# Moving operands read in two halves by turns, 16 columns at a time, with operands moved to whole 64-byte lines

## The reference, cut to what matters

```python
def first_block(...):
    n = _rmsnorm(h, pre_mix_norm[l])
    proj = jnp.einsum('btd,dn->btn', n, w_in[l])
    ...
    merged = (sigmoid(gate_a) * einsum('btv,vd->btd', y_gdn, w_branch_gdn[l])
              + sigmoid(gate_b) * einsum('btv,vd->btd', y_dsa, w_branch_dsa[l]))
    mix = jnp.einsum('btd,de->bte', merged, w_out[l])
    h = h + _rmsnorm(mix, post_mix_norm[l])
    n2 = _rmsnorm(h, pre_mlp_norm[l])
    u = jnp.square(jax.nn.relu(jnp.einsum('btd,df->btf', n2, w_up[l])))
    h = h + _rmsnorm(jnp.einsum('btf,fd->btd', u, w_down[l]), post_mlp_norm[l])

def swiglu(x, w_gu, w_down):
    gu = jnp.einsum('bsd,df->bsf', x, w_gu)
    g, u = gu[..., :D_FF_2], gu[..., D_FF_2:]
    return jnp.einsum('bsf,fd->bsd', jax.nn.silu(g) * u, w_down)

def moe_swiglu(x, w_router, w_gu, w_down):          # N_EXPERTS = 8, TOP_K = 2
    ...
    for e in range(N_EXPERTS):
        out = out + gates[..., e:e + 1] * swiglu(x, w_gu[e], w_down[e])
    return out
```

## Time and profile before

| | before |
|---|---|
| median of the runs | 1777.97 us |
| the profiled execution | 1777.92 us, of which the span is 1776.1 us |
| PE busy | 1754.1 us (99%), 11249 matmuls and as many loads |
| DVE busy | 1363.0 us (77%) |
| ACT busy | 1076.1 us (61%) |
| POOL busy | 158.2 us (9%) |
| DMA | 447.90 MB, 252 GB/s over the span |
| mean granted TensorE clock | 0.996 of 2.4 GHz |

### The profile page before, as it was taken

The page is one execution under the profiler, slowest core; times in us unless marked ns, Lnnn a source line. Parts: engine busy times, 40 slices in busy tenths (PEclk is TensorE's granted clock), DMA queues, the critical chain, the costliest instruction groups (busy, mean ns, idle before and its releaser), DMA issues.

```text
span 1776.1 us, 26513 instructions
## 1 busy us (share of the span) xinstructions
PE 1754.1 (99%) x11249; PEld 1579.0 (89%) x11249; DVE 1363.0 (77%) x1591; ACT 1076.1 (61%) x1200; POOL 158.2 (9%) x165
## 2 busy tenths in 40 slices
PE   9999999999999999999999999999999999999997
PEld 8999999999988999998998888888888888888885
DVE  6895598577664667655687899888889898889897
ACT  7754455455544454444446777777777776767774
POOL 1454270000000100000030100000000000000110
PEclk9999999999999999999999999999999999999999
DMA  9342464656556555575463599999999999999994
GB/s 288 119 116 64 124 184 143 211 180 189 181 188 202 190 164 167 183 235 178 132 201 130 202 380 376 380 336 383 372 381 341 385 370 384 332 381 376 379 390 171
DMA packets 265206, 447.90 MB, mean 252 GB/s; under 512 B 11461, under 2 KB 135848, under 8 KB 264952
## 3 DMA queue, kind: packets, MB, share of 16 engines
q1 hardware_dynamic: 263464, 440.36, 71.1%
q0 software_dynamic: 1616, 5.77, 0.8%
HBM read 438.99 MB, written 4.73 MB: 250 GB/s over the span
## 4 chain that ended last, share of the span: by engine, by line
PE 91%; DVE 5%; ACT 2%; issue 1%; DMA 0%; SPq 0%; DVEq 0%; ACTq 0%
PE bank L428 27%; PE bank L430 27%; PE bank L429 27%; DVE ring_r L418 2%; PE bank L3240 1%; ACT hi_ring L403 1%; PE bank L2522 1%; PE bank L3154 1%; PE bank L1348 1%; PE bank L1340 1%; DVE arena L923 1%; PE bank L1832 1%; PE bank L2503 0%; PE bank L2152 0%; PE bank L1817 0%
## 5 line engine op out<-in xcount | busy, mean ns | idle before, releaser
L418 DVE TENSOR_TENSOR ring_r<-ring,hi_ring 128x2048 fp32r<-128x2048 f32 x401 | 905.4, 2284 | 264.7 <-ACT hi_ring L403 264.2
L403 ACT CAST hi_ring<-ring 128x2048 fp32r<-128x2048 f32 (+1 forms) x404 | 757.2, 1904 | 136.3 <-PE bank L430 129.3
L428 PE MATMUL bank<-hi_ring,arena_r 128*128 128x512 f32 (+1 forms) x1526 | 569.2, 373 | 2.0 <-DVE ring_r L418 2.0
L429 PE MATMUL bank<-ring_r,arena_r 128*128 128x512 f32 (+2 forms) x1534 | 567.5, 370 | 0.0
L430 PE MATMUL bank<-hi_ring,arena_r 128*128 128x512 f32 (+1 forms) x1526 | 566.7, 371 | 0.0
L428 PE MATMUL bank<-ring_r,hi_ring 128*128 128x256 f32 (+1 forms) x1400 | 398.9, 285 | 0.0
L430 PE MATMUL bank<-ring_r 128*128 128x256 f32 (+1 forms) x1400 | 395.2, 282 | 0.0
L429 PE MATMUL bank<-ring_r,hi_ring 128*128 128x256 f32 (+1 forms) x1400 | 395.0, 282 | 0.0
L428 PEld LDWEIGHTS bank<-hi_ring,arena_r 128*128 128x128 f32 x1526 | 286.8, 188 | 54.9 <-DVE ring_r L418 4.8
L429 PEld LDWEIGHTS bank<-ring_r,arena_r 128*128 128x128 f32 (+1 forms) x1534 | 287.9, 188 | 51.0
L430 PEld LDWEIGHTS bank<-hi_ring,arena_r 128*128 128x128 f32 x1526 | 286.9, 188 | 50.2
(11 more groups left out here) (436 smaller groups left out, 1572.7 us busy)
## 6 DMA issues: line engine op xcount, KB each, us to landing
ring<-in_w_gu_moe SPq DMA_DIRECT2D x176, 1024.0 KB, 7.3
ring<-in_w_down_moe SPq DMA_DIRECT2D x88, 1024.0 KB, 6.0
ring<-in_w_in SPq DMA_DIRECT2D x31, 1024.0 KB, 5.5
ring<-in_w_gu_dense SPq DMA_DIRECT2D x22, 1024.0 KB, 5.2
ring<-in_w_up SPq DMA_DIRECT2D x16, 1024.0 KB, 5.5
ring<-in_w_down SPq DMA_DIRECT2D x16, 1024.0 KB, 5.0
ring<-in_w_in_a SPq DMA_DIRECT2D x10, 1024.0 KB, 5.8
ring<-in_w_down_dense SPq DMA_DIRECT2D x10, 1024.0 KB, 5.0
```

The lines of the kernel that those rows point to most:

```text
L403: q.e.copy(hi_ring[:, b:b + m], ring[:, a:a + m]).then_inc(*q.did(("hi", of.tag, i)))
L418: q.e.tensor_tensor(ring_r[:, a:a + m], ring[:, a:a + m], hi_ring[:, b:b + m].bitcast(F32), ALU.subtract).then_inc(*q.did(("lo", of.tag, i)))
L428: q.e.matmul(ps, a[0], b[0], start=first, stop=False)
L429: q.e.matmul(ps, a[0], b[1], start=False, stop=False)
```

## The change

`mm3` gives the moving operand and the PSUM output another order of columns. `paired_lines` cuts the columns into two halves, and takes 16 of the first half, 16 of the second, the next 16 of the first, and so on (where their number is a multiple of 128: the shapes 256 and 512, not 272). Every column still goes to its own place in PSUM. 16 columns are 64 bytes.

The other edits move operands. `ARN` grows by 8 columns, so `ring` and `hi_ring` begin 32 bytes later, at 110144: a whole multiple of 64, and 64 past a multiple of 256, and so do all weight blocks. The operands in `arena` that meet weights now begin 192 bytes past a multiple of 256 (for `yg`: 4224 + 4 x 2128 = 12736 = 49 x 256 + 192), and so does `X`, which becomes two packed arrays of 8 x 256 columns, where it had rows of 272. So the moving and the stationary operand of a matmul lie 128 bytes apart modulo 256. Two kinds are exceptions: `nX` keeps its rows of 272 columns, 1088 bytes, so that its distance to the weights goes through 64, 128, 192 and 0 with k in the 256-column shape; and `memT` against two blocks of stationary weights in `arena`.

```diff
-ARN = 26472
+ARN = 26480
...
-    X = Pair(nX.hi[:, :, 0:SEQ], nX.lo[:, :, 0:SEQ])
+    X = Pair(*[shaped(ring_r[:, o:o + 8 * SEQ], (8, SEQ)) for o in (NRAW * BLK + 32, NRAW * BLK + 32 + 8 * SEQ)])
...
+    def paired_lines(a):
+        return a.rearrange("p (h j e) -> p j h e", h=2, e=16) if a.shape[1] % P == 0 else a
+
     def mm3(q, ps, a, b, first, last):
-        q.e.matmul(ps, a[0], b[0], start=first, stop=False)
-        q.e.matmul(ps, a[0], b[1], start=False, stop=False)
-        return q.e.matmul(ps, a[1], b[0], start=False, stop=last)
+        ps, high, low = [paired_lines(v) for v in (ps, b[0], b[1])]
+        q.e.matmul(ps, a[0], high, start=first, stop=False)
+        q.e.matmul(ps, a[0], low, start=False, stop=False)
+        return q.e.matmul(ps, a[1], high, start=False, stop=last)
...
-    yg = pair_at(2176, 8, SEQ)
+    yg = pair_at(2128, 8, SEQ)
...
-    yd = pair_at(8576, 8, SEQ)
+    yd = pair_at(8528, 8, SEQ)
...
-    mg, xin2 = pair_at(13056, 8, SEQ), at(17152, 2, 1024)
+    mg, xin2 = pair_at(13008, 8, SEQ), at(17152, 2, 1024)
...
-    u_, dn = pair_at(2048, 32, SEQ), at(18432, 2, 1024)
+    u_, dn = pair_at(2064, 32, SEQ), at(18456, 2, 1024)
...
-    mix2 = pair_at(6656, 8, SEQ)
+    mix2 = pair_at(6608, 8, SEQ)
...
-    gg = pair_at(6656, 22, SEQ)
+    gg = pair_at(6608, 22, SEQ)
...
-    xs2 = pair_at(10648, 8, 2 * P)
-    hh, hp = at(14744, 2816), pair_at(17560, 22, P)
+    xs2 = pair_at(10640, 8, 2 * P)
+    hh, hp = at(14736, 2816), pair_at(17552, 22, P)
```

More of the change, by code:

```diff
@@ L532, in emit @@
     wT, vn, ktm = AT, D, AT[:, 0:8, :]
-    yg = pair_at(2176, 8, SEQ)
+    yg = pair_at(2128, 8, SEQ)
     rhT, hn = at(6272, P)[0:16, :], [at(o, 512) for o in (13056, 13568, 14080, 16768)]
     sq2 = [flat(AT[:, 2 * j:2 * j + 2, :]) for j in range(8)]
-    aq = at(6528, 8, SEQ)
-    yd = pair_at(8576, 8, SEQ)
+    aq = at(6480, 8, SEQ)
+    yd = pair_at(8528, 8, SEQ)
     iq, ik, ak, av = at(19456, 4, SEQ), at(22528, T), at(22800, 2, T), at(14896, 3, 256)
@@ L551, in emit @@
     mix_sq, x2_sq, r_mix, r_x2 = at(12672, 2, 4), at(12680, 2, 2), at(12684, 2), at(12686, 2)
-    u_, dn = pair_at(2048, 32, SEQ), at(18432, 2, 1024)
-    ut = [at(18432 + SEQ * j, SEQ) for j in range(4)]
-    dn_gain, dn_junk, dn_sq, r_dn = at(21248, 1024), at(20992, 256), at(22272, 2, 4), at(22280, 2)
+    u_, dn = pair_at(2064, 32, SEQ), at(18456, 2, 1024)
+    ut = [at(18456 + SEQ * j, SEQ) for j in range(4)]
+    dn_gain, dn_junk, dn_sq, r_dn = at(21272, 1024), at(21016, 256), at(22296, 2, 4), at(22304, 2)
     xr, xv = at(0, 2, 1024), at(2048, 2, 1024)
@@ L565, in emit @@
     cos2, sin2 = C[:, later + 520:later + 776], C[:, later + 776:later + 1032]
-    mix2 = pair_at(6656, 8, SEQ)
+    mix2 = pair_at(6608, 8, SEQ)
     kx, vx = at(10752, 6, SEQ), at(12288, 2, 12 * 65)
-    memT, memin = pair_at(22376, 8, SEQ), at(2176, 2, 1024)
+    memT, memin = pair_at(22352, 8, SEQ), at(2176, 2, 1024)
     mk_raw = [at(2048, 8, P), at(14368, 8, P)]
@@ L571, in emit @@
     mv_raw = [at(18944, 4, SEQ), at(21304, 4, SEQ)]
-    mv_later = [Pair(at(6656 + 1024 * h, 4, SEQ, of=arena_r), at(o, 4, SEQ, of=arena_r)) for h, o in ((0, 18944), (1, 21304))]
-    ang, kf = at(20480, SEQ), at(20736, SEQ)
+    mv_later = [Pair(at(6608 + 1024 * h, 4, SEQ, of=arena_r), at(o, 4, SEQ, of=arena_r)) for h, o in ((0, 18944), (1, 21304))]
+    ang, kf = at(20504, SEQ), at(20760, SEQ)
     qm = at(13856, 2, SEQ)
@@ L583, in emit @@
     lg, m8b, gt2, oh = at(8192, 2, 8), at(8208, 2, 8), at(8224, 2, 8), at(8240, 2, 2, 8)
-    ixf, sel, ge, posm, cnt = at(8272, 2, 8), at(8288, 2, 8), at(8304, 2, 8), at(8320, 2, 8), at(8336, 8)
+    ixf, sel, ge, posm, cnt = at(9232, 2, 8), at(9176, 2, 8), at(9192, 2, 8), at(9208, 2, 8), at(9224, 8)
     lgT = at(8344, SEQ)
@@ L587, in emit @@
     gs = at(9112, 8)
-    ST = [at(9624 + 256 * j, SEQ, of=arena_r) for j in range(4)]
-    xs2 = pair_at(10648, 8, 2 * P)
-    hh, hp = at(14744, 2816), pair_at(17560, 22, P)
+    ST = [at(9616 + 256 * j, SEQ, of=arena_r) for j in range(4)]
+    xs2 = pair_at(10640, 8, 2 * P)
+    hh, hp = at(14736, 2816), pair_at(17552, 22, P)
     acc, moe_gains = at(2048, 2, 1024), at(0, 2, 1024)
```

## The result

| | before | changed |
|---|---|---|
| median | 1779.08 us (4 runs beside it) | 1822.7 us (4 runs, 1820.7 to 1823.8) |
| ratio | | 1.0243, 95% interval 1.023 to 1.0256 |
| span of the profiled execution | 1776.1 us | 1820.7 us |

The account below looks back on a forecast made before the run. PE's start-to-start matmul distance was taken as the bound; gains of 14.9 (experts), 7.2 (other row products) and 21.1 us (256 columns) made 43.2, times 0.91 39 us, so 1777.9 - 39 = 1739 us, range 1680 to 1786.

Parts of the forecast that it names:

- What bounds the kernel: Whole kernel: time is, to nine tenths, PE's matmul count times start-to-start distance; PE holds 91% of the chain.
- 0.91: Factor on the summed gain, as 9% of the chain lies on other engines and in waits: 43.2 to 39 us.
- the order in halves: mm3's 256- and 512-column matmuls: turns hold the reads' distance, gaining 1.9 to 8.1 ns each, taken as 5.0.
- In step at 128 bytes: Moving read and stationary load under turns: both advance alike, holding 128 bytes, so extra time from meeting goes away.
- The lines: 702 512-column row products outside the experts: starting on 64-byte lines gains 5.3 ns each, 3.7 us.
- The rival of the jumps: Reading and PSUM writing jump every 16 columns, each costing one column's time, 0.417 ns: 1861 us; chance 0.07.
- The rival "the reads never met": PE's moving and load reads: extra time is the same in any order; 1774 to 1778 us; chance 0.22.
- The rival of the bad distance: SBUF reads: memory repeats every 128 bytes, so in-step reads meet all the time; 1814 us; chance 0.11.
- The cheaper order: mm3: turning also removes what 512 columns pay without a load, reaching 213.3 ns; 1687 us; chance 0.18.
- the two slower rivals: Bad distance (1814 us) and jumps (1861 us), left out of the range; chance 0.18 together.
- The readings ahead of the sum: PE's extra time per matmul: 272 columns take 124.2 ns beside a 24-column load, 126.1 beside 128; load costs 1.9.

Follow-up runs that it names:

- order_only: The kernel before with only the turns between halves, all operands in their old places; 1822.9 us, ratio 1.0247.
- read_turns: The changed kernel with only the moving operand read by turns from the halves, PSUM written in one contiguous piece; 1824.6 us, ratio 1.0249.
- apart_64: The changed kernel with columns in contiguous order and the rings moved so ring and arena operands lie 64 bytes apart modulo 256; 1773.6 us, ratio 0.9965.
- write_turns: The changed kernel with the moving operand read contiguously and only PSUM written by turns in the halves; 1789.5 us, ratio 1.0053.
- quarters: The changed kernel with four quarters by turns, 16 columns from each, instead of two halves; 1803.5 us, ratio 1.0135.
- best_x192: apart_0 with X placed 192 bytes from the stationary weights modulo 256; 1763.5 us, ratio 0.9918.
- best_x64: apart_0 with X placed 64 bytes from the stationary weights modulo 256; 1765.9 us, ratio 0.9922.
- apart_0: The changed kernel with columns in contiguous order and the rings moved so ring and arena operands begin at the same place modulo 256; 1772.1 us, ratio 0.9959.
- places_only: The changed kernel with mm3 as before, so old column order in the new operand places; 1789.5 us, ratio 1.0055.

## Why the prediction was wrong

1739 us with a range of 1680 to 1786 was forecast, and 1822.7 measured; the sign was wrong.

- **What bounds the kernel** was right: the start-to-start distance of `mm3` is the time, and nothing else moved. 46.1 us worked out from distances stand against 43.6 us measured: 0.95 of what PE's matmuls lost arrived, where 0.91 was forecast.
- **The step that failed** is "the order in halves": that it can only gain, between 1.9 and 8.1 ns for each matmul, taken as 5.0. It measured a loss, against contiguous order in the same places, of 7.3 ns at 512 columns and 1.6 at 256. The reasoning looked at what the turns take away, the changing distance of the two reads, and priced the turns themselves at nothing in the sum. `order_only` shows that they alone make 240 ns whatever the distance, and `read_turns` that it is the reading.
- **In step at 128 bytes** was built on the idea that reads which meet cost time. Under the turns, distances of 64, 128 and 160 all gave 240.0 ns; under contiguous order distances do matter, but 128 is among the worst at 512 columns. The sign named for it, longer matmuls on `nX` at k = 3 and 7 where the distance is 0, is absent: the mean distance up to such a matmul is 119.4 ns, and 119.8 to 120.7 at the other k.
- **The lines.** The 5.3 ns between the experts and the row products were put down, with a doubt, to the 64-byte line. The distance accounts for it: 64 in one and 160 in the other. `apart_64` on whole lines has the experts' old 229 ns in the row products too (229.2), which are 5.0 ns better than before there, so the size was near right and the cause wrong. That 160 by itself costs what it did is inferred from the 233 ns at 128 and 192: no run has 160 on whole lines, and no run shows a line of 64 bytes at all. The changed kernel's 128 costs the experts 3.6 ns by itself under contiguous order, which the sum had at nothing.
- **The rival of the jumps** came nearest in cause, at a chance of 0.07, and is right only in that reading by jumps costs. Its price, one column's time for each run of 16, is 13.3 ns at 512 columns and 6.7 at 256, 1861 us; measured are 7.3 and 1.6 ns, more than four to one where its sign was two to one, and no fixed price for a jump fits the other runs. It also took PSUM writing for a cause. The Trainium skill's rule (Advanced Engine Details and Errata, PSUM Cachelines) that any output that isn't contiguous slows matmuls does not hold here: `write_turns` costs nothing with runs of 16. The other half of that rule, neighbours two by two are enough, agrees.
- **The rival "the reads never met"** had the Trainium skill's two independent read ports behind it (SBUF — State Buffer, Who interferes with whom). For contiguous order the measurement decides against that rule as a statement on speed: the same 512-column matmuls with the same loads take 227.4 to 233.3 ns, by where the operands lie alone.
- **The rival of the bad distance** (1814 us) was near in time by luck and wrong in cause: `order_only` has the same loss at other distances. It and the rival of the jumps were also summed without the 0.91 that the gains got; with it they are 1810 and 1853 us.
- **The cheaper order** (0.18) has nothing for it: no order tried is faster than contiguous, and no 512-column mean is under 227.3 ns, where it asked for 213.3.
- **The range** left out the two slower rivals for their small chance, 0.18 together, and the measured time lies between them.
- **The readings ahead of the sum** were fair, but read past: 11 of 12.8 ns were there beside loads of 24 columns too. That hinted that most of the extra time doesn't hang on the load's length, and so that an edit to the reading could lose as well as win. The row was used for a lower bound of a gain.

What stays open: why runs of 64 columns are free, of 32 and fewer not, and why quarters cost less than halves; whether the load beside a matmul has a part in what the turns cost, as no run has them without it; by what structure of the memory distances 0 to 192 take the order that they do; and what picks the pace that a stretch of 256-column matmuls keeps. The runs show sizes, not a mechanism.

## What to carry to other kernels

Where PE is bound by matmuls back to back, let the moving operand be read in runs of at least 64 float32 columns; an output in PSUM cut into runs of 16 cost nothing here. Measure the distance from start to start, not busy time, and try the address of the moving operand against the stationary one in steps of 64 bytes: here places alone were worth 0.8% (`best_x192`, with `X` packed), and each shape had its own best distance. Look at more than one stretch of each shape, and at several runs: one kernel can hold two paces. A row that shows extra time in the very thing that an edit changes is a reason to price the edit on both sides of zero.

## What the runs showed of the hardware that I had not expected

- Read by turns from two halves in runs of 16, float32r matmuls of 512 columns take 18 ticks for 16 columns, 240.0 ns, at every place tried, and those of 256 columns 120.0 ns but for stretches at 123.3 (144 matmuls in the changed kernel, some 1180 in `read_turns`). Contiguous reads take 227.3 to 233.3 ns for 512 columns.
- The distance of the two operands, in steps of 64 bytes from 0 to 192, moves a contiguous 512-column matmul by 6 ns (2.6%) and one of 256 columns on `X` in the dense layer from 118.8 ns at 128 bytes to 113.3 at 192 (4.6%).
- A stretch of 256-column matmuls keeps its pace for hundreds of them, and the same shape at the same distance can keep another one elsewhere in the kernel: 113.3 and 117.8 ns in `best_x64`, 120.0 and 118.7 in `apart_0`.
- PSUM took outputs in runs of 16 columns with half an operand between neighbours at no cost (`write_turns` and `places_only`, 1789.5 us both).
